# Four modulation chunks of a layer move from TensorE's delta stage to GpSimd, and their products with ones into the output projection

## What is computed

```python
def first_block(x, c, ...):
    for l in range(2):
        mod = silu(c) @ w_ada[l] + b_ada[l]              # 6 groups of 1024: sh1, sc1, gt1, sh2, sc2, gt2
        h = rms_norm(x, norm_mix[l]) * (1 + sc1) + sh1
        p = h @ w_in[l]                                  # qkv, z, b, a, sw_q, sw_k, sw_v, gate_a, gate_b
        q, k, v = silu(causal_dwconv(qkv))               # q and k with l2_norm
        o_dn = gated_delta_rule_chunked(q, k, v, g, beta)
        y_a = (rms_norm(o_dn) * silu(z)) @ w_dn_out[l]
        y_b = swa_sink_attention(rope(sw_q), rope(sw_k), sw_v) @ w_swa_out[l]
        x = x + gt1 * ((sigmoid(gate_a) * y_a + sigmoid(gate_b) * y_b) @ w_o[l])
        h = rms_norm(x, norm_ffn[l]) * (1 + sc2) + sh2   # sh2 is group 3
        x = x + gt2 * ((silu(conv(h @ w_up_a)) * (h @ w_up_b)) @ w_down[l])
```

## Time and profile before

| what | value |
|---|---|
| median of 3 runs | 2354.92 us (2351.8 to 2355.92) |
| the profiled execution, its own time | 2355.41 us |
| its span from first to last instruction | 2353.6 us |
| mean granted TensorE clock | 0.973 of 2.4 GHz |
| PE busy | 2227.0 us (95%) |
| DVE busy | 1508.2 us (64%) |
| ACT busy | 1062.2 us (45%) |
| POOL busy | 491.2 us (21%) |

### The profile page before, as it was taken

The page is one execution under the profiler, slowest core; times in us unless marked ns, Lnnn a source line. Parts: engine busy times, 40 slices in busy tenths (PEclk is TensorE's granted clock), DMA queues, the critical chain, the costliest instruction groups (busy, mean ns, idle before and its releaser), DMA issues.

```text
span 2353.6 us, 39957 instructions
## 1 busy us (share of the span) xinstructions
PE 2227.0 (95%) x17369; PEld 2127.3 (90%) x17369; DVE 1508.2 (64%) x1868; ACT 1062.2 (45%) x1346; POOL 491.2 (21%) x238
## 2 busy tenths in 40 slices
PE   7996999999999979999999999989999999989999
PEld 7995789899989868898999999978999999878999
DVE  6855576677668357667666555686556555786554
ACT  2654265433355533644335344545434434645433
POOL 0822004599436310058300000000000000000000
PEclk7999999999999989999999999989999999999999
DMA  8761044677657311466555556424555556423653
GB/s 281 247 192 41 1 144 144 215 261 231 209 177 233 108 36 54 144 197 215 180 179 177 182 185 192 126 72 145 189 186 167 191 180 189 134 90 126 193 184 126
DMA packets 332856, 383.81 MB, mean 163 GB/s; under 512 B 12551, under 2 KB 315402, under 8 KB 332554
## 3 DMA queue, kind: packets, MB, share of 16 engines
q1 hardware_dynamic: 332234, 381.10, 50.5%
q10 hardware_dynamic: 448, 0.16, 0.0%
HBM read 380.19 MB, written 1.05 MB: 162 GB/s over the span
## 4 chain that ended last, share of the span: by engine, by line
PE 78%; DVE 11%; ACT 6%; issue 3%; DMA 1%; POOL 0%; SPq 0%; ACTq 0%; DVEq 0%
PE bank L720 16%; PE bank L722 16%; PE bank L721 16%; PE bank L943 5%; PE bank L944 5%; PE bank L945 5%; DVE weights_low L1348 4%; ACT weights_high L2056 3%; DVE arena L1450 1%; PE bank L734 1%; PE bank L997 1%; PE bank L1006 1%; PE bank L982 1%; PE bank L1132 1%; PE bank L758 1%
## 5 line engine op out<-in xcount | busy, mean ns | idle before, releaser
L1348 DVE TENSOR_TENSOR weights_low<-ring,weights_high 128x2048 fp32r<-128x2048 f32 x302 | 742.9, 2460 | 461.2 <-ACT weights_high L2056 461.0
L720 PE MATMUL bank<-h_high,weights_high 128*128 128x256 f32 x3296 | 943.9, 286 | 24.0 <-DVE weights_low L1348 15.6
L721 PE MATMUL bank<-h_low,weights_high 128*128 128x256 f32 x3296 | 928.6, 282 | 0.0
L722 PE MATMUL bank<-h_high,weights_low 128*128 128x256 f32 x3296 | 928.3, 282 | 0.0
L2056 ACT ACTIVATE weights_high<-ring 128x2048 fp32r<-128x2048 f32 x302 | 578.1, 1914 | 711.9 <-PE bank L722 520.7
L720 PEld LDWEIGHTS bank<-h_high,weights_high 128*128 128x128 f32 x3296 | 623.5, 189 | 39.7 <-DVE weights_low L1348 22.9
L721 PEld LDWEIGHTS bank<-h_low,weights_high 128*128 128x128 f32 x3296 | 624.5, 189 | 3.0 <-issue 2.9
L722 PEld LDWEIGHTS bank<-h_high,weights_low 128*128 128x128 f32 x3296 | 624.1, 189 | 0.0
L943 PE MATMUL bank<-hidden_high,weights_high 128*128 128x256 f32 x1056 | 300.2, 284 | 1.6 <-DVE hidden_low L1589 1.2
L944 PE MATMUL bank<-hidden_low,weights_high 128*128 128x256 f32 x1056 | 299.4, 284 | 0.0
L945 PE MATMUL bank<-hidden_high,weights_low 128*128 128x256 f32 x1056 | 299.3, 283 | 0.0
(11 more groups left out here) (427 smaller groups left out, 2928.8 us busy)
## 6 DMA issues: line engine op xcount, KB each, us to landing
ring<-in_w_in SPq DMA_DIRECT2D x80, 1024.0 KB, 5.3
ring<-in_w_up SPq DMA_DIRECT2D x44, 1024.0 KB, 5.3
ring<-in_ffn_w_gate SPq DMA_DIRECT2D x44, 1024.0 KB, 5.3
ring<-in_ffn_w_up SPq DMA_DIRECT2D x44, 1024.0 KB, 5.4
ring<-in_ffn_w_down SPq DMA_DIRECT2D x44, 1024.0 KB, 4.9
side<-in_w_ada SPq DMA_DIRECT2D x42, 1024.0 KB, 7.7
ring<-in_w_down SPq DMA_DIRECT2D x22, 1024.0 KB, 5.0
ring<-in_w_dn_out SPq DMA_DIRECT2D x8, 1024.0 KB, 5.3
```

The lines of the kernel that those rows point to most:

```text
L720: mm(o[:, m, :], a_, high[:, t, :], start=(t == 0), stop=False)
L721: mm(o[:, m, :], a_, low[:, t, :], start=False, stop=False)
L722: last = mm(o[:, m, :], b_, high[:, t, :], start=False, stop=(t == KT - 1))
L1348: v.tensor_tensor(low, wide(q), high.bitcast(F32), ALU.subtract).then_inc(chunk_split, 1)
```

## The change

Group 3's four chunks of each layer are treated as the other groups' are. `mod_pair`, `copy_mod` and the semaphore `mod_copied` are gone. GpSimd does two side sums between the squares and the head normalisation, and two between the off-diagonal masks and the output squares. `mod_reduce(l, 3)` stands behind the first dno chunk on TensorE, and `modulation(l, 3)` behind the first merge product on VectorE. Since the reduction uses a bank of the alternating pair, the second dno chunk now has the same bank as the first.

```diff
-ADR_AFTER = {("swq", 2): 2, ("swq", 3): 3, ("wo", 3): 4}
+ADR_AFTER = {("swq", 2): 2, ("dno", 0): 3, ("wo", 3): 4}
...
-        rope_bank = [L[1 - R["adr", l, 3] % 2] for l in range(LAYERS)]
+        rope_bank = [L[R["swq", l, 3] % 2] for l in range(LAYERS)]
...
-                if g == 3:
-                    pe.wait_ge(mod_copied, 2 * l + 2)
-                elif PREV["adr", l, g] is not None:
+                if PREV["adr", l, g] is not None:
                     pe.wait_ge(*release(PREV["adr", l, g]))
...
-            def mod_pair(l, pair):
...
-                for half in range(2):
-                    j = SIDE.index((l, 12 + 2 * pair + half))
-                    pe.wait_ge(side_landed[j % 2], 16 * (j // 2 + 1))
-                    w = side[j % 2][:, :].rearrange("p (t n) -> p t n", t=KT)
-                    for t in range(KT):
-                        last = mm(L[r % 2][:, half * T:(half + 1) * T], ccol[:, t:t + 1].to_broadcast([P, P]), w[:, t, :], start=(t == 0), stop=(t == KT - 1))
-                    last.then_inc(side_summed, 1)
...
                 rope_sum_late(l, 4)
-                mod_pair(l, 0)
-                mod_pair(l, 1)
...
-                    else:
-                        mod_reduce(l, 3)
                     rope_turn_late(l, 2 * k_)
...
                 for i in range(4):
                     linear3(("dno", l, i), oH, oL)
+                    if i == 0:
+                        mod_reduce(l, 3)
...
-                modulation(l, 3)
                 copy_steps(0, 10)
...
                     v.tensor_tensor(mrg[:, 2 * i:2 * i + 2, :], LV[R[key] % 2], gab[:, 2 * i:2 * i + 2, :], ALU.mult).then_inc(merged, 1)
+                    if i == 0:
+                        modulation(l, 3)
...
-                copy_mod(0)
                 act.wait_ge(blocks_inverted, l + 1)
...
-                copy_mod(1)
                 for k_ in range(3):
...
                     g_.tensor_tensor(HSQ[:, i, :].rearrange("p (m t) -> p m t", m=2), qq, qq, ALU.mult).then_inc(head_squared, 1)
+                for j in (6 + 24 * l, 7 + 24 * l):
+                    side_sum(j)
                 for n in range(8 * l, 8 * l + 8):
...
+                for j in (8 + 24 * l, 9 + 24 * l):
+                    side_sum(j)
                 pool.wait_ge(step_copied, 12 * l + 12)
...
-                pool.wait_ge(mod_summed, 6 * l + 4)
                 pool.wait_ge(out_split, 4 * l + 4)
```

More of the change, by code:

```diff
@@ L422, in build @@
         blocks_inverted = sem("blocks_inverted")
-        mod_copied = sem("mod_copied")
         kv_ready = sem("kv_ready")
@@ L983, in mod_reduce @@
                 last.then_inc(mod_summed, 1)
-            def mod_pair(l, pair):
-                r = R["adr", l, 3]
-                if pair == 0:
-                    pe.wait_ge(*release(PREV["adr", l, 3]))
-                else:
-                    pe.wait_ge(mod_copied, 2 * l + 1)
-                for half in range(2):
-                    j = SIDE.index((l, 12 + 2 * pair + half))
-                    pe.wait_ge(side_landed[j % 2], 16 * (j // 2 + 1))
-                    w = side[j % 2][:, :].rearrange("p (t n) -> p t n", t=KT)
-                    for t in range(KT):
-                        last = mm(L[r % 2][:, half * T:(half + 1) * T], ccol[:, t:t + 1].to_broadcast([P, P]), w[:, t, :], start=(t == 0), stop=(t == KT - 1))
-                    last.then_inc(side_summed, 1)
             def weigh_start(c, w, used):
@@ L2284, in _ @@
                         sums[0] += 1
-                def copy_mod(pair):
-                    act.wait_ge(side_summed, 24 * l + 8 + 2 * pair)
-                    a_(acc[:, 1, 512 * pair:512 * pair + 512], L[R["adr", l, 3] % 2][:, :], ACT.Copy, scale=1.0 / P).then_inc(mod_copied, 1)
                 def copy_back(k_, g):
```

## The result

The changed kernel takes 2361.48 us (median of 6 runs, 2358.09 to 2362.49) against 2352.95 us for the kernel before beside it (2346.69 to 2355.92). The ratio is 1.0037, with a 95% interval of 1.0023 to 1.0052: **slower, by 0.37%**. The forecast was 2352.7 with a range up to 2358.5, and a slower kernel had a chance of 0.10. The profiled execution has a span of 2360.0 us (2353.6 before) at a mean granted clock of 0.969 (0.973).

What follows compares the result with a forecast made beforehand. The prediction took TensorE as the bounding chain over most of the kernel. Its terms summed to -1.0 us in the first layer and -1.2 in the second, together -2.2, giving 2352.7 us against the 2354.92 median; range 2346.0 to 2358.5.

Steps and rivals of the forecast that it cites:

- The products leave the path: Delta stage: inversion transposes wait only for ScalarE's last placement, not the modulation products; -5.4 us first layer, -5.6 second.
- nothing else holds them there: Delta stage: besides ScalarE's placement nothing delays the inversion's transposes, as VectorE has written its placements by then; supports -5.4, -5.6 us.
- The reductions leave the stage: Delta stage, before the rotary turn: ScalarE's copy, TensorE's wait and 1.92 us of reductions go; -3.1 us a layer.
- the clock: TensorE in the delta stage: half clock after idling costs +2.1 us a layer; a later clock fall disappears, -1.1.
- The fall at the rotary turn: Delta stage, 245.5 to 248.5 us: half clock behind the wait and reductions, taken as gone; -1.1 us a layer.
- the cold start: Start of the inversion: TensorE, idle without the products, runs 4.1 us at half clock; +2.1 us a layer.
- GpSimd's work, behind: First two inversion levels: side sums stretch five VectorE rotary instructions by 0.59 each, plus L1686; +3.3 us a layer (0 to 4.9).
- GpSimd's work, ahead: End of qkv, start of z: side sums stretch two VectorE splits on the path; +1.5 us a layer (0 to 4.0).
- the 0.74 a split: VectorE's 128x2048 weight splits beside GpSimd, priced from first-FFN rows: +0.74 us each (0 to 2.0).
- The reductions arrive in the projection: Output projection, between first and second dno chunks: reductions join TensorE's gapless chain, hiding the bank wait; +1.7 us a layer.
- VectorE is held to the worst: Rival: splits before z and rotary instructions stretch fully, 8.9 us a layer instead of 4.8; 2360.9 us, chance 0.10.
- GpSimd gives way: Rival: part or all of VectorE's stretching doesn't come; 2347.9 us at half, 2343.1 at none; chance 0.33.

## Why the prediction was wrong

It had the sign of every term right, but the sum wrong: -2.2 us where +8.5 was measured. The means over the traces (six stretches of the changed kernel, two of the kernel before) put the miss in these places.

- **The products leave the path (-5.4, -5.6).** The transposes did start within 0.1 us of ScalarE's placement. But the term was read as if that placement would stay where it was. The step that failed is "nothing else holds them there". The placement ended 70.5 and 71.1 us after the head normalisation in the kernel before, and 73.0 in the mean in the changed one, where more of the preparation ran at half clock. The preparation takes 73.0 us, against 76.4 before: -3.4, so 2 us a layer are missing. Why the clock falls there more often stays open. The prediction also took the second layer to repeat the first nearly to the hundredth; its preparation was 0.8 us longer before the change already.
- **The reductions leave the stage (-3.1) and the clock (+2.1, -1.1).** In the kernels with the two sums behind cut the levels are 62.0 us in the mean, against 64.3 before: -2.3 where these three terms make -2.1. So they are not part of the miss, by some luck. The fall at the rotary turn went, and the cold start came. But the forecast looked only at the clock at the two places that the edit touches. The second fall of the kernel before, 30 us later, it never read, and it stayed. With the products kept, moving the reductions takes both falls away and gains 6.2 and 6.4 us, where the same two terms make 4.2.
- **GpSimd's work, behind (+3.3).** 66.5 against 62.0 is 4.5, at the upper end of the range for this term (0 to 4.9). 3.6 of it are TensorE's waits, in both layers of the trace that isolates them; the rest, about 1 us, isn't accounted for. The mechanism was right. The reasons for the size were partly off: not five instructions of +0.59, but three tensor-tensors of +0.97 to +1.58 and the two L1666 of +1.97 and +0.41, some of it in slack. The step that failed is the price of a stretched instruction, taken from the mean and the worst of rows in the FFN (1.28 and 1.52 us): in the four instructions that show it, the price was about the rest of the GpSimd instruction then running, and those last up to 2.7 us here. The levels as a whole became 2.2 us longer in the mean (66.5 against 64.3) where -3.1 + 2.1 - 1.1 + 3.3 = +1.2 was forecast: 1 us a layer.
- **GpSimd's work, ahead (+1.5).** +2.9 and +4.4 in the first traces. Over all traces, the first head normalisation stands at 161.9 us in the mean of six with whole sums ahead (161.2 to 162.9) and at 159.5 in twelve without (158.3 to 161.0). From layer one's third side sum to layer two's head normalisation it is 362.4 us in the six with (361.8 to 362.8), and 357.9 in the twelve without (355.1 to 359.4). So 2.4 and 4.5 (the latter with the 0.8 that the first comparison put down to the FFN). The step that failed is the 0.74 a split, taken as mean minus median of splits in another place, the FFN, many of which lay only partly beside a side sum. Here they lie beside it whole, and cost +0.83, and over 1 each for the pair behind, in layer two 1.6 to 1.7. 3.9 us in all.
- **The reductions arrive in the projection (+1.7).** 2.4. Seven of the eight products with ones are 1.4 of it; the step that failed counted VectorE's modulation, which stands ahead of a split there, and the bank at nothing. 0.7 us a layer.

Together 2 x (2 + 1 + 0.7) + 3.9 = 11.3 us, against 8.5 + 2.2 = 10.7 by the medians. The rival "VectorE is held to the worst" had the sign and the place, and its 2360.9 is within 1 us of the measured time. That is in part luck: it put the whole miss on contention, 17.8 us for both layers where the forecast had 9.6. Cutting the sums gave 14 us by the medians, and 17 by the ratios, so 4.8 to 7.4 of the 10.7 us missed are contention; the rest is the clock in the preparation and the projection. The rival "GpSimd gives way", to which 0.33 went, fell: every split on the path ahead was stretched. The range had no case in which the clock of a stretch that the edit doesn't touch moves, although six runs of the kernel before lie 9 us apart.

## What to carry to other kernels

Work taken off a critical engine is worth its time less what its absence costs: here the chunk products cost 5 to 6 us a layer on TensorE and kept its clock up for 2.4 of that, and GpSimd's version of them held VectorE for more than the rest, 7 us a layer. To price such work, look at the length of GpSimd's single instructions: a VectorE instruction with two SBUF operands was held here for about what was left of one, up to 1.97 us of 2.67. Before moving the large part, move the smallest edit alone: eight one-column products, put where TensorE waited anyway, gave 0.66% by themselves, and nothing that GpSimd did added to it. The side job on GpSimd was free only where VectorE read from PSUM or idled and where GpSimd's own next result wasn't due; both had to be true at once, and the kernel with all four sums late failed on the second.

## What the runs showed of the hardware

- Beside GpSimd tensor-tensors, a 128x512 VectorE tensor-tensor with both operands in SBUF went from 0.69 us to 1.66, 1.75 and 2.27, and a scalar-tensor-tensor from 0.75 to 2.72 and 1.16; two others, L1672 at 244.19 and at 260.47 us, kept 0.69. Those with one operand in PSUM stayed at 0.67 to 0.69 between them. I had bounded the small ones by 1.52.
- Four of these five ended 0.55 us behind the GpSimd instruction that was running when they began (246.64, 249.39, 251.07 and 256.35 us).
- With a few products of one column, and the wait ahead of them, in the levels, TensorE's clock was at half for 3.4 us right there, and for 3.4 or 6.8 us again some 30 us later; with them moved away and all other products kept, the whole stretch of 58 us was at 1.00 in six of six stretches.
- TensorE's granted clock in one program varies between its executions: preparations of 70.5, 72.0, 74.6 and 75.6 us for the same instructions, with 0.84 granted over one of 70.5 us and 0.77 over the one of 75.6.
